# Second branch's gate for token block 1 computed beside the last four gated-unit tile pairs of a hybrid encoder block

## What is computed

```python
u = a_in * jax.nn.sigmoid(a_gate)
u = lax.conv_general_dilated(u, conv_w[l][:, None, :], ...) + conv_b[l]
u = jax.nn.silu(_layernorm(u, conv_ln_g[l], conv_ln_b[l]))
y_b = u @ conv_w_pw2[l]

merged = jax.nn.sigmoid(ga) * y_a + jax.nn.sigmoid(gb) * y_b
x = x + merged @ w_out[l]

h2 = _rmsnorm(x, norm2_g[l]).reshape(B * S, D)
x = x + _peer(h2, peer_w_q[l], peer_keys[l], peer_u[l], peer_v[l]).reshape(B, S, D)
```

## Time and profile before

| What | us |
|---|---|
| median of 3 runs (lowest, highest) | 4389.01 (4383.09, 4396.44) |
| the profiled execution's own time | 4385.64 |
| its span on the core | 4383.2 |
| PE busy (products) | 3739.1 (85%) |
| DVE busy | 2675.1 (61%) |
| ACT busy | 888.1 (20%) |
| POOL busy | 774.1 (18%) |
| bytes moved by DMA | 1530.99 MB, mean 349 GB/s |

### The profile page before, as it was taken

How to read it: one execution, slowest core, us unless ns; L and a number is a source line. 1 busy time by engine, 2 the same in 40 slices (tenths; PEclk the granted TensorE clock), 3 DMA queues, 4 the chain that set the end, 5 groups by cost and what they waited for, 6 DMA issues and landing times. The chain is left out here.

```text
span 4383.2 us, 39792 instructions
## 1 busy us (share of the span) xinstructions
PE 3739.1 (85%) x13700; PEld 2252.1 (51%) x13700; DVE 2675.1 (61%) x3938; ACT 888.1 (20%) x2061; POOL 774.1 (18%) x525
## 2 busy tenths in 40 slices
PE   8999999999999999766699697858888887777776
PEld 3444479445666667663687586334444442222222
DVE  2232258102899999865777877876656764545544
ACT  1232310101122212242111111122212222212111
POOL 0000000000133332332221212222212222212111
PEclk9999999999999999888899898979999999999999
DMA  3112248887899999999999999999999999999998
GB/s 131 58 58 68 68 166 301 300 312 272 329 365 376 385 417 412 408 405 406 426 425 427 423 417 427 422 390 427 401 418 416 414 393 421 424 427 428 429 429 352
DMA packets 142776, 1530.99 MB, mean 349 GB/s; under 512 B 15313, under 2 KB 21585, under 8 KB 22097
## 3 DMA queue, kind: packets, MB, share of 16 engines
q0 software_dynamic: 73728, 1073.77, 58.6%
q1 hardware_dynamic: 66960, 444.62, 26.8%
q10 hardware_dynamic: 1984, 11.31, 0.7%
HBM read 1525.45 MB, written 4.19 MB: 349 GB/s over the span
## 5 line engine op out<-in xcount | busy, mean ns | idle before, releaser
L1695 PE MATMUL bank<-arena_h,wring 128*128 128x128 f32 (+5 forms) x6720 | 1391.9, 370 | 131.2 <-DVE arena_h L1430 40.8
L1695 PEld LDWEIGHTS bank<-arena_h,wring 128*128 128x128 f32 x6720 | 1031.1, 195 | 487.8 <-issue 184.8
L613 POOL DMA_INDIRECT arena_c<-in_peer_uv,arena_c x256 | 506.2, 1977 | 2528.6 <-DVE arena_o L1362 1371.7
L1353 DVE SCALAR_TENSOR_TENSOR arena_c<-arena_c 128x2048 f32<-128x2048 f32 x256 | 585.4, 2287 | 185.6 <-DMA arena_c<-in_peer_uv,arena_c 185.4
L2045 PE MATMUL bank<-arena_c,arena_h 128*128 128x512 f32 x1024 | 479.1, 612 | 159.5 <-ACT arena_h L993 159.5
L1362 DVE SCALAR_TENSOR_TENSOR arena_o<-arena_c,arena_o 128x2048 f32<-128x2048 f32 x234 | 549.4, 2348 | 68.0 <-ACT arena_c L803 61.5
L2010 PE MATMUL bank<-arena_c,cols 128*128 128x512 f32 x1024 | 481.2, 614 | 113.7 <-ACT cols L951 91.1
L1607 DVE SCALAR_TENSOR_TENSOR arena_c<-arena_c 128x2048 f32<-128x2048 f32 x128 | 293.4, 2292 | 316.7 <-DMA arena_c<-in_peer_uv,arena_c 316.5
L801 ACT ACTIVATE arena_c<-arena_c 128x1 f32<-128x1 f32 x384 | 77.8, 203 | 1939.7 <-DVE arena_c L1353 1428.5
L626 POOL DMA_INDIRECT arena_c<-in_peer_uv,arena_c x256 | 265.8, 1038 | 1049.7 <-PE bank L2010 537.8
L1564 DVE SCALAR_TENSOR_TENSOR arena_c<-arena_c 128x2048 f32<-128x2048 f32 x128 | 293.5, 2293 | 239.4 <-DMA arena_c<-in_peer_uv,arena_c 237.7
(11 more groups left out here) (215 smaller groups left out, 2699.0 us busy)
## 6 DMA issues: line engine op xcount, KB each, us to landing
wring<-in_w_in SPq DMA_DIRECT2D x176, 1024.0 KB
wring<-in_w_out SPq DMA_DIRECT2D x48, 1024.0 KB
wring<-in_peer_w_q SPq DMA_DIRECT2D x48, 1024.0 KB
wring<-in_gla_w_o SPq DMA_DIRECT2D x32, 1024.0 KB
wring<-in_conv_w_pw SPq DMA_DIRECT2D x32, 1024.0 KB
wring<-in_w_v SPq DMA_DIRECT2D x16, 1024.0 KB
wring<-in_w_ga SPq DMA_DIRECT2D x16, 1024.0 KB
wring<-in_w_o_quarters SPq DMA_DIRECT2D x16, 1024.0 KB
```

The lines of the kernel that those rows point to most:

```text
L613: pool.indirect_dma_start(out=slot_of(n), out_offset=None, in_=uv_tab, in_offset=at)\
L1353: V.scalar_tensor_tensor(row, row, 1.0, block_of(h2, n // P), ALU.mult, ALU.mult, accum_out=act_u[:, n % TOP:n % TOP + 1]).then_inc(dotted, 1)
L1695: last = M(ps[bank][:, at:at + hi - lo], w_tile(slot)[:, k, :], act_in[:, k, lo:hi], start=k == 0, stop=k == KT - 1)
```

## The change

It moves branch B's gate for block 1 into `ma1`. A pair becomes 6 tiles: 2 of branch B's gate (into the second half of the same PSUM bank), 2 of branch A's gate, 2 of `w_o`; ACT's `mb1_gates` reads them just before `ma1_gates`. The 16 separate tiles and their `mb1_gate` calls are gone. No tile is added or dropped. The turns become 10, 10, 11, 10, 10, 10, 11, 10 steps (before 10, 11, 11, 10, 9, 9, 9, 8), so that the convolution ends at step 86 (before 81). The LayerNorm begins 1 step after that (before 3), the projection of branch B at step 96 (before 95), the norm at 111 (before 110); `QUERY1_AT` stays 115.

```diff
-SB_MA1_LAST = SB_MA1 + 36
-SB_GB1 = SB_MA1_LAST + 8
-SB_PW1 = SB_GB1 + 16
+SB_MA1_LAST = SB_MA1 + 48
+SB_PW1 = SB_MA1_LAST + 12
...
-TURN_AT = (4, 14, 25, 36, 46, 55, 64, 73, 81)
+TURN_AT = (4, 14, 24, 35, 45, 55, 65, 76, 86)
 OG_AT = (4, 7)
-IT_AT = (2, 5)
-X1_AT = 80
-GB_AT = 79
-XC_AT, SQUARE_AT = 84, 85
-RSTD_AT, ROOT_AT, RECIP_AT = 89, 89, 90
-SCALE1_AT, SILU1_AT = 91, 91
-PW_AT = 95
-SCALE2_AT, SILU2_AT = 96, 97
-RES1_AT = (103, 105, 107, 109)
-NORM1_AT = 110
+IT_AT = (3, 6)
+X1_AT = 84
+XC_AT, SQUARE_AT = 87, 88
+RSTD_AT, ROOT_AT, RECIP_AT = 92, 92, 93
+SCALE1_AT, SILU1_AT = 94, 94
+PW_AT = 96
+SCALE2_AT, SILU2_AT = 97, 98
+RES1_AT = (104, 106, 108, 110)
+NORM1_AT = 111
 QUERY1_AT = 115
...
             def mb1_gates(n):
                 p = pair["mb1"]
-                act.wait_ge(p["gate"], n + 1)
-                A(sgb1[:, 2 * n:2 * n + 2, :], two(4 + n % 4, P), ACT.Sigmoid).then_inc(p["sig"], 1)
+                act.wait_ge(pair["ma1"]["gate"], n + 1)
+                gates = ps[6 - 2 * (n % 2)][:, 2 * P:4 * P].rearrange("p (m t) -> p m t", t=P)
+                A(sgb1[:, 2 * n:2 * n + 2, :], gates, ACT.Sigmoid).then_inc(p["sig"], 1)
...
                     if j >= 4 and r + 1 in IT_AT:
+                        mb1_gates(2 * (j - 4) + IT_AT.index(r + 1))
                         ma1_gates(2 * (j - 4) + IT_AT.index(r + 1))
...
-                if 0 <= s - GB_AT < 4:
-                    mb1_gates(s - GB_AT)
...
-                if 0 <= s - (SQUARE_AT + 1) < 4:
-                    mb1_gates(4 + s - (SQUARE_AT + 1))
...
                 pe.wait_ge(p["use"], count)
-                two_tiles(first, i, per, hT, 6 - 2 * a, P, 2 * P).then_inc(p["gate"], 1)
-                two_tiles(first + 2, i, per, oT, 7 - 2 * a, P, 2 * P).then_inc(p["val"], 1)
+                two_tiles(first, i, per, hT, 6 - 2 * a, P, 2 * P, 2 * P)
+                two_tiles(first + 2, i, per, hT, 6 - 2 * a, P, 2 * P).then_inc(p["gate"], 1)
+                two_tiles(first + 4, i, per, oT, 7 - 2 * a, P, 2 * P).then_inc(p["val"], 1)
...
-            for n in range(4):
-                mb1_gate(n)
             pe.wait_ge(pair["glu1"]["use"], 2 + KT)
             pe.wait_ge(cv1_done, KT)
...
-                mb1_gate(4 + n)
```

More of the change, by code:

```diff
@@ L558, in _ @@
                 for a in range(2):
[L559 to L562, removed]
+                    loads(SB_MA1 + 6 * a, j, 16, w_in, j * 4 + (WGB + 2 * a), 2)
+                    loads(SB_MA1 + 6 * a + 2, j, 16, w_in, j * 4 + (WGA + 2 * a), 2)
+                    loads(SB_MA1 + 6 * a + 4, j, 16, w_o, j * 4 + 2 * a, 2)
+                loads(SB_MA1 + 12, j, 16, w_in, j * 2 + (WGATE + 10), 2)
+                loads(SB_MA1 + 14, j, 16, w_in, j * 2 + (WGLU + 10), 2)
             for a in range(2):
-                loads(SB_MA1_LAST + 4 * a, 0, 8, w_in, WGA + 12 + 2 * a, 2)
-                loads(SB_MA1_LAST + 4 * a + 2, 0, 8, w_o, 12 + 2 * a, 2)
-            row_loads(SB_GB1, w_in, WGB)
+                loads(SB_MA1_LAST + 6 * a, 0, 12, w_in, WGB + 12 + 2 * a, 2)
+                loads(SB_MA1_LAST + 6 * a + 2, 0, 12, w_in, WGA + 12 + 2 * a, 2)
+                loads(SB_MA1_LAST + 6 * a + 4, 0, 12, w_o, 12 + 2 * a, 2)
             row_loads(SB_PW1, w_pw2, 0)
@@ L1769, in _, with two_tiles @@
             pe.wait_ge(ot_ev, HEADS * 4)
-            def two_tiles(first, i, per, act_in, bank, lo, hi):
+            def two_tiles(first, i, per, act_in, bank, lo, hi, at=0):
                 for m in range(2):
                     tile_ready(first + m, i, per)
-                    last = project(first + m, act_in, bank, lo, hi, m * (hi - lo))
+                    last = project(first + m, act_in, bank, lo, hi, at + m * (hi - lo))
                 return last
@@ L1918, in _ @@
                 for a in range(2):
-                    ma1(SB_MA1 + 4 * a, j, 12, a, j * 2 + (a + 1))
-                glu1(SB_MA1 + 8, j, 12, 5, j)
+                    ma1(SB_MA1 + 6 * a, j, 16, a, j * 2 + (a + 1))
+                glu1(SB_MA1 + 12, j, 16, 5, j)
             for a in range(2):
[L1922 to L1927, removed]
+                ma1(SB_MA1_LAST + 6 * a, 0, 12, a, 6 + a + 1)
             pe.wait_ge(pair["ma1"]["use"], 2 + 8)
-            for n in range(4):
-                mb1_gate(n)
             pe.wait_ge(pair["glu1"]["use"], 2 + KT)
```

## The result

| | before | after |
|---|---|---|
| median of 4 runs | 4388.39 us (4383.09 to 4396.44) | 4434.25 us (4427.85 to 4438.51) |
| profiled execution, span | 4383.2 us | 4436.8 us |

The ratio is 1.0102, with a 95% interval of 1.0087 to 1.0118: the change makes the kernel 46 us slower. The forecast was 4423, in a range of 4387 to 4450. The profiled execution of after is the slowest of its four, 4438.51 us, so the two traces lie 53 us apart where the medians lie 46 apart.

A forecast was written before the change was run, and what follows sets the result against it. It took the DMA engines at 426 GB/s to bound the kernel from step 115 on, so only shortfall before it counts: 0.5 + 31 + 5.5 = +37 us on 4385.6 gives 4422.6, taken as 4423, range 4387 to 4450.

The forecast's parts named there:

- The forecast's case: Whole kernel: slower than before, at 4423 us; slower was given 0.80.
- The ledger: Up to step 115: time is bytes at 426 GB/s plus the DMA engines' shortfall; a delay there carries to the end.
- Turns 0 to 3: Convolution's first turns: DVE waits about 1.5 us at step 24, step 45 starts near 1503; shortfall +0.5 us.
- Turns 4 to 7: Ten loads at 6.1 us before each gated unit, turns of 99.5 us, step 86 at 1889; shortfall +31 us.
- the gated units' 40 us: Turns 4 to 7: idle DMA time lies here, when ring and slots are full and DVE stands still.
- the 8 to 20 given as a sign: Turns 5 to 7: DVE waits 8 to 20 us in total per turn, before the take or second merge.
- The reason given for 99.5: Turns 4 to 7: 101 us a turn, or 98 if loads go faster while DVE waits; 99.5 taken.
- both queues always full: Rival, turns 4 to 7: weights get a third of 426 GB/s, 7.4 us a load; 4475 us, chance 0.04.
- LayerNorm: Step 86 to branch B's first merge: 63 us, DVE waits 3 us for the mean; shortfall 13.5 against 8.0, +5.5 us.
- To step 115: Projection, w_out and norm: same tiles and merges one step later, costed at nothing; one step, 5 us, if wrong.
- 2130 was given as a sign: Step 115 starts near 2130 us, and from there the same steps follow.

The follow-up runs named there:

- e6: After with the pairs' merges one step earlier in turns 4 to 7 (steps 2 and 5 instead of 3 and 6); 4408.81 us, 1.0042 times before.
- e1: After's gate tiles inside the pairs, but before's turn lengths and merges at steps 2 and 5; 4412.99 us, 1.0052 times before.
- e7: After with the pairs' merges later (steps 4 and 8 of a turn instead of 3 and 6); 4427.42 us, 1.0089 times before.
- e5: After without the 16 gate tiles' loads, the products made from branch A's gate tiles instead; 4366.92 us (one run).
- e4: After with the 16 gate tiles loaded but only one of the 16 products of each made; 4431.03 us (one run).
- e8: Before with one gate tile behind each output-gate tile in turns 0 to 3, and 13 steps a turn there; 4377.84 us, 0.9976 times before.
- e3: After with a turn's four gate tiles between the gated unit's tiles, the last four behind the last pair; 4410.76 us, 1.0052 times before.

## Why the prediction was right

The forecast's case came true; the sum was 13 us short, +37 against +50.5 in the ledger.

- **The ledger.** It held. 50.4 of the profiled 52.9 us are made by step 115. For all kernels that move the same bytes, the time from step 4 to step 115 less the shortfall is 850 to 853 us; this is arithmetic as long as the bytes are the same. What the runs add is that a lead or lag made before step 115 stays: from there to the end of the span all kernels take 2284 to 2290 us.
- **Turns 0 to 3:** said +0.5, came +2.6. The take at step 24 waits 1.18 us (1.5 said), and step 45 starts at 1501.7 (1503 said).
- **Turns 4 to 7,** said +31, came +41.4. **This is the term that was mis-sized.** Its mechanism is what the rows show: ten loads set the distance, then PE takes four tiles in 40 us while the DMA engines run at 333. Said: 61 us a phase, 6.1 a load, and three turns of 99.5. Came: 64.1, 60.1 and 62.1 us, 186.4 for 30 loads, 6.2 each, and gated units of 41.4, 41.6 and 39.8 us (the end of each overlaps the next tile's start by 0.2); together 308.9 against 298.5. These 10.4 us have three parts of nearly one size: 3.9 because 99.5 was taken where 61 + 39.8 make 100.8, 3.4 for the loads, 3.1 for the gated unit. Turn 7 took 94.1 from its first pair, not 90. Step 86 starts at 1902.9 against 1889. (That these 10.4 us equal the ledger's is chance: the whole stretch is 401.2 us long against 386, and 150.4 MB came in it against 149.)
- **Where the idle DMA time lies.** The prediction named only the gated units' 40 us. They hold 28 of the 48 us. 11 more lie at the end of turn 7, which has no gated unit behind it, where PE has no tile to take and DVE has just waited at the last merge; as a place of idle DMA time it was not named. DVE's waits are 24 and 29 us in turns 5 and 6, more than the 8 to 20 given as a sign, and 17 in turn 7.
- **The reason given for 99.5,** that loads go faster while DVE waits, is right in kind and was wrong for this table. After's DVE waits late, at the merge of step 6 (17.33 us in turn 6) and in the gated unit. e6 and e1 wait early, and there loads do take 4.7 to 5.3 us in turns 5 and 6 (6.0 and 5.9 in turn 4). The forecast used one price for a load, from a kernel in which DVE hardly waited (4 us in turns 4 to 7), and could not have given e1, e6 or e7.
- **Against the rival "both queues always full"** I held that it needs DVE to wait for gathers. That is wrong. In turn 5 PE's tiles from 1638.34 to 1667.88 start 7.39, 7.39, 7.39 and 7.37 us apart (the rows of the result), and so do these of turn 6, while the dots wait 0.0: DVE lives on the gathers already in its slots. In the stretch of the next rows a gather took 14.7 us from issue to landing and POOL issued one each 7 to 8 us, so two were under way at a time (an estimate from these two figures).

```profile
1742.88 5.47 PE L1692 MATMUL bank<-arena_h,wring 128*128 128x128 f32 x32 [2.94 <-DMA wring<-in_w_in]
1750.27 5.47 PE L1692 MATMUL bank<-arena_h,wring 128*128 128x128 f32 x32 [1.92 <-DMA wring<-in_w_in]
1757.66 3.84 PE L1692 MATMUL bank<-arena_o,wring 128*128 128x128 f32 x32 [1.92 <-DMA wring<-in_gla_w_o]
1765.04 6.59 PE L1692 MATMUL bank<-arena_o,wring 128*128 128x128 f32 x32 [3.54 <-DMA wring<-in_gla_w_o]
```

  The queues then (1742 to 1766; packets, MB, share):

```profile
q0 software_dynamic: 457, 6.60, 64.5%
q1 hardware_dynamic: 491, 3.62, 36.0%
```

  Weights get 35% of the bytes. Over 1609 to 1638, with DVE just out of its wait, they got more than half:

```profile
q1 hardware_dynamic: 886, 6.47, 56.9%
q0 software_dynamic: 336, 4.98, 40.5%
```

  So a phase has a fast part, at 1.05 MB x 29/6.47 = 4.7 us a tile, and a part in which both queues are full, at 7.39; the 6.2 lies between the two. A tile and a gather of 2.10 MB are 3.15 MB, which at 426 GB/s is 7.4 us. The Trainium skill (DMA: Bandwidth & Descriptors, Queues, rings and completion order) says that each engine takes one packet from each queue in turn; where both are full, these rows agree with it, and the rival was half right: its rate was real, for part of each phase.
- **LayerNorm:** said 63 us, 13.5 short, a wait of 3 us for the mean; came 62.6, 14.3 and 2.62.
- **To step 115:** costed at nothing, and 6.8 stands beside 6.8. Step 115 starts at 2146.4, where 2130 was given as a sign.
- **e5 and e4** show that PE's twelve tiles were no term: with the products gone the kernel is 3 us faster, within the spread, with the loads gone 67.

The gates alone make e1 24 us slower than before, the table alone 5, both together 46: some 16 us come only from the two together, and e6 shows that in the table it is the later merges that make them. The cause of what e8 loses in its last stretch stays open.

## What to carry to other kernels

Where a stretch near the end always runs the DMA engines full, judge a move by the time in which they fall short of that rate, stretch by stretch, and put added loads where another engine sets the pace and they are short of it (e8), not where they are full, even if an engine has gaps beside them. A burst of loads before a long tile costs the burst at a shared rate and then the idle queue behind it; the price of a load depends on what else is asked for meanwhile. An engine that must wait for the burst in any case should wait early, so that it doesn't ask for transfers that compete with what it waits for, and does ask for them in the long tile behind (e6: 25 us from one line of a table). That is no rule for every place: where no long tile follows, as in turn 7, waiting late or not at all was better (e7).

## What the runs showed of the hardware

- With the gather queue and the weight queue both full, weight tiles of 1.05 MB came 7.39 us apart (after, 1638 to 1668 and 1743 to 1765); just after DVE had stood at the take, when the gathers moved 4.98 MB in 29 us and not 7.60 in 30, they came at 4.7 us (after, 1609 to 1638).
- The gated unit's two value tiles come 9.9 us apart. So where DVE is at the take before the first is done, it waits 9.32 us for the second: twice in after, and the 28.0 us behind PE in e1's, e3's and e7's takes are three times this.
- The gated unit took 41.4 and 41.6 us in turns 4 and 5 of after, where PE had waited 3.46 and 1.91 us just before it, and 39.8 in turn 6, where it began without a wait. The difference lies at its start: in its first 4 us the granted clock is 0.64, 0.57 and 1.00, 1.0 being 2.4 GHz, and its first ten instructions take 4.6, 4.9 and 3.1 us. A wait just before does not always bring this: behind 1.31 us (e7), 2.31 (before) and 3.52 (e8) the clock in the same 4 us is 1.00 and the unit takes 40 us. Which waits bring it these rows do not tell.
